# Output-weight maxima moved into the third head and a wait, last squares cut in two, residual rows loaded earlier

## The reference: what is computed

```
o = rms_norm(o_f + o_b, norm_g)          # per head of 128, HGRN2 group, 4 heads
o = o * silu(hgate)
y = concatenate([o_hg, o_att]) @ w_out   # (1152 x 1024) @ (1024 x 1024)
x = layer_norm(ALPHA * x + g2 * y, ln_g[1], ln_b[1])
x = layer_norm(ALPHA * x + 0.5 * g3 * swiglu(x * (1 + sc3) + sh3, ...), ln_g[2], ln_b[2])
```

## Time and profile before

| | |
|---|---|
| median of 3 runs | 2874.22 us (2873.36 to 2875.57) |
| the profiled execution | 2877.72 us, its span 2875.8 us |
| PE busy | 2614.7 us (91%) |
| DVE busy | 1979.7 us (69%) |
| ACT busy | 814.0 us (28%) |
| mean granted TensorE clock | 0.951 of full |

### The profile page before, as it was taken

How to read it: one execution, slowest core, us unless ns; L and a number is a source line. 1 busy time by engine, 2 the same in 40 slices (tenths; PEclk the granted TensorE clock), 3 DMA queues, 4 the chain that set the end, 5 groups by cost and what they waited for, 6 DMA issues and landing times. The chain is left out here.

```text
span 2875.8 us, 37783 instructions
## 1 busy us (share of the span) xinstructions
PE 2614.7 (91%) x15240; PEld 1631.2 (57%) x15240; DVE 1979.7 (69%) x2871; ACT 814.0 (28%) x1196; POOL 158.4 (6%) x191
## 2 busy tenths in 40 slices
PE   6899999999998867888699999868989999999996
PEld 6655555555554656766566666533545555555553
DVE  2577777778668666777455765668787777777768
ACT  0511111111211436666442242231311121111220
POOL 0000000000000220111200110101100000000003
PEclk9999999999998989999799999879999999999998
DMA  6323222322112110000110100022111111111001
GB/s 228 103 81 95 93 92 95 99 92 88 44 53 67 52 43 1 1 1 1 35 39 12 35 16 38 26 77 83 47 58 48 48 46 44 44 44 44 29 15 66
DMA packets 147786, 159.79 MB, mean 56 GB/s; under 512 B 8087, under 2 KB 125107, under 8 KB 146626
## 3 DMA queue, kind: packets, MB, share of 16 engines
q1 hardware_dynamic: 147650, 157.89, 17.2%
HBM read 147.74 MB, written 10.12 MB: 55 GB/s over the span
## 5 line engine op out<-in xcount | busy, mean ns | idle before, releaser
L1303 PE MATMUL psum<-act_hi,ffn_win_hi 128*128 128x384 f16 x2112 | 691.6, 327 | 2.0 <-DVE ffn_h_even L1610 2.0
L1303 PE MATMUL psum<-act_lo,ffn_win_hi 128*128 128x384 f16 x2112 | 691.4, 327 | 0.0
L1303 PE MATMUL psum<-act_hi,ffn_win_lo 128*128 128x384 f16 x2112 | 691.3, 327 | 0.0
L1474 ACT ACTIVATE ffn_silu<-psum,ffn_win_inverse 128x384 f32<-128x384 f32 x132 | 76.4, 579 | 1040.7 <-PE psum L1303 1038.8
L1645 DVE SCALAR_TENSOR_TENSOR Y<-psum,ffn_h_unit,Y 128x512 f32<-128x512 f32 x342 | 253.2, 749 | 120.9 <-PE psum L1334 118.9
L1334 PE MATMUL psum<-ffn_wout_hi,ffn_h_hi 128*128 128x512 f16 x792 | 309.1, 390 | 22.9 <-DVE Y L1128 12.3
L1334 PE MATMUL psum<-ffn_wout_hi,ffn_h_lo 128*128 128x512 f16 x792 | 308.3, 389 | 0.0
L1334 PE MATMUL psum<-ffn_wout_lo,ffn_h_hi 128*128 128x512 f16 x792 | 308.3, 389 | 0.0
L1303 PEld LDWEIGHTS psum<-act_hi,ffn_win_hi 128*128 128x128 f16 x2112 | 207.6, 98 | 138.6 <-DVE ffn_h_even L1610 2.4
L1303 PEld LDWEIGHTS psum<-act_hi,ffn_win_lo 128*128 128x128 f16 x2112 | 207.4, 98 | 138.1 <-issue 2.5
L1303 PEld LDWEIGHTS psum<-act_lo,ffn_win_hi 128*128 128x128 f16 x2112 | 207.5, 98 | 136.8 <-issue 2.3
(11 more groups left out here) (325 smaller groups left out, 4433.2 us busy)
## 6 DMA issues: line engine op xcount, KB each, us to landing
ffn_win_raw<-in_w_in SPq DMA_DIRECT2D x88, 512.0 KB, 5.1
w_mod<-in_w_mod SPq DMA_DIRECT2D x36, 1024.0 KB, 5.0
ffn_wout_raw<-in_w_out SPq DMA_DIRECT2D x44, 512.0 KB, 4.1
scan_w_raw<-in_w_mix SPq DMA_DIRECT2D x20, 512.0 KB, 5.3
x_after<-Y SPq DMA_DIRECT2D x9, 512.0 KB, 2.6
mixout_residual<-x_after SPq DMA_DIRECT2D x9, 512.0 KB, 3.4
Y<-in_x_sample SPq DMA_DIRECT2D x8, 512.0 KB, 6.7
ffn_residual<-in_x_sample SPq DMA_DIRECT2D x8, 512.0 KB, 3.3
```

The source lines that it names most:

```text
L1303: last = nc.tensor.matmul(bank[:, 0:CH], win[b][w][:, half, k, :], K.A[a][:, k, c * CH:(c + 1) * CH], start=(n == 0), stop=(n == 3 * KT - 1))
L1474: nc.scalar.activation(sa[s][:], pa[s][:, 0:CH], ACT.Silu, scale=winv[:, b:b + 1]).then_inc(silu, 1)
```

## The change

Five edits, all without a change of what is computed. (1) The maxima of output-weight blocks 0, 2, 3 and then 1, 4 are taken in the third head, those of 5, 6, 7 behind the last head. (2) A new `last_norm` replaces `norm` for the last head: it multiplies by the gate first, takes the three maxima and makes the weights' powers of two, and then waits for the root. (3) ACT squares the last head's first 768 tokens before the last tile is in, and PE's third unit waits for the second part. (4) The residual tiles have a place of their own (that of `ffn_wout_gated`, which is first written later), and tiles 0 and 1 are loaded right behind the first rows. (5) The second norm's rows are waited for and scaled behind tile 5 instead of ahead of tile 0.

```diff
@@ class MixOut @@
         for v in range(2):
             sp.dma_start(self.gate[:, v, :], ...).then_inc(self.rows, 16)
         sp.dma_start(self.gR[:], K.ln_g[0:1, :].broadcast_to([P, D])).then_inc(self.rows, 16)
         sp.dma_start(self.bR[:], K.ln_b[0:1, :].broadcast_to([P, D])).then_inc(self.rows, 16)
+        for t in range(2):
+            self.load_residual(sp, t)
 
     def load_late(self, sp):
         sp.wait_ge(self.w_lo, KT)
-        for t in range(2):
-            self.load_residual(sp, t)
         sp.dma_start(self.gB[:], ...).then_inc(self.affine_rows, 16)
         sp.dma_start(self.bB[:], ...).then_inc(self.affine_rows, 16)
...
     def splits_hi(self, act):
-        act.wait_ge(self.w_scale, 1)
...
     def splits(self, dve):
-        link(nc.vector.tensor_scalar(self.wq[:].bitcast(I32), self.wmax.bitcast(I32), EXPONENT, None, ALU.bitwise_and))
-        link(nc.vector.tensor_scalar(self.wq[:], self.wq[:], TINY, FULL, ALU.max, ALU.mult))
-        link(nc.vector.tensor_tensor(self.otops[:], self.omax, self.wq[:], ALU.mult))
+        link(nc.vector.tensor_tensor(self.otops[:], self.omax, self.wq, ALU.mult))
         nc.vector.tensor_reduce(self.otop[:], self.otops[:], AX_X, ALU.max).then_inc(self.o_max, 1)
-        nc.vector.reciprocal(self.ws[:], self.wq[:]).then_inc(self.w_scale, 1)
...
         dve.wait_ge(self.rows, 64)
-        dve.wait_ge(self.affine_rows, 32)
-        for rows in (self.gR, self.bR, self.gB, self.bB):
+        for rows in (self.gR, self.bR):
             link(nc.vector.tensor_scalar(rows[:], rows[:], ALPHA, None, ALU.mult))
...
             self.residual(dve, t + 3)
-            if c == 1:
+            if c == 0:
+                dve.wait_ge(self.affine_rows, 32)
+                for rows in (self.gB, self.bB):
+                    self.link(self.nc.vector.tensor_scalar(rows[:], rows[:], ALPHA, None, ALU.mult))
+            else:
                 self.affine(dve, 0)
             self.unit(dve, t + 2)
@@ hgrn_phase @@
+        mix_parts = ((0, 2, 3), (1, 4), (5, 6, 7))
...
                 for c in range(NCH):
+                    if h == HGH - 1 and c == NCH - 1:
+                        pe.wait_ge(sq_s, h + 2)
...
             def squares(h):
+                cut = 2 * CH if h == HGH - 1 else 0
+                if cut:
+                    act.wait_ge(oe_s, h * RPH + RPH)
+                    nc.scalar.activation(nb[:, 0:cut], acc[:, 0:cut], ACT.Square).then_inc(sq_s, 1)
                 act.wait_ge(oe_s, h * RPH + RPH + 1)
-                nc.scalar.activation(nb[:], acc[:], ACT.Square).then_inc(sq_s, 1)
+                nc.scalar.activation(nb[:, cut:], acc[:, cut:], ACT.Square).then_inc(sq_s, 1)
...
+            def last_norm(h):
+                dve.wait_ge(sq_s, h + 2)
+                link(nc.vector.scalar_tensor_tensor(acc[:], acc[:], K.cols[:, C_HGN + h:C_HGN + h + 1], K.O[:, h, :], ALU.mult, ALU.mult))
+                link(mix_weight_max(2))
+                link(nc.vector.tensor_scalar(K.mix_wq.bitcast(I32), K.mix_wmax.bitcast(I32), EXPONENT, None, ALU.bitwise_and))
+                link(nc.vector.tensor_scalar(K.mix_wq, K.mix_wq, TINY, FULL, ALU.max, ALU.mult))
+                link(nc.vector.reciprocal(K.mix_ws, K.mix_wq))
+                dve.wait_ge(rs_s, h + 1)
+                link(nc.vector.tensor_tensor(K.O[:, h, :], acc[:], nb[:], ALU.mult))
+                link(out_max(h))
...
                 row_max(n + 1, 0, V_, F0)
-                mix_weight_max(h, 0, 1)
+                if h == HGH - 2:
+                    mix_weight_max(0)
                 states(h, 0, 1, 0, 1)
...
                 gates(n, 0)
-                mix_weight_max(h, 6)
+                if h == HGH - 2:
+                    mix_weight_max(1)
                 states(h, 1, 1, 2, 3)
```

More of the change, by code:

```diff
@@ L2831, in out_max, with mix_weight_max @@
                 for k in tiles:
-                    largest(nc, K.mix_omax[:, k:k + 1], K.O[:, k, :])
-            def mix_weight_max(h, *tiles):
-                if h < HGH - 1:
-                    return
-                for k in tiles:
-                    dve.wait_ge(mix_in[k // NBLK], 16 * (KT - NBLK if k >= NBLK else NBLK))
-                    largest(nc, K.mix_wmax[:, k:k + 1], K.mix_raw[k][:])
+                    last = largest(nc, K.mix_omax[:, k:k + 1], K.O[:, k, :])
+                return last
+            def mix_weight_max(part):
+                dve.wait_ge(mix_in[part], 16 * len(mix_parts[part]))
+                for k in mix_parts[part]:
+                    last = largest(nc, K.mix_wmax[:, k:k + 1], K.mix_raw[k][:])
+                return last
+            def last_norm(h):
[8 more added lines that the diff above has]
+                link(out_max(h))
             def scan_head(h):
@@ L2917, in _ @@
                 scan_head(h)
-            norm(HGH - 1)
+            last_norm(HGH - 1)
 def rope_tables(np):
@@ L2970, in program @@
                  for k in range(KT)]
-    K.mix_omax, K.mix_wmax = K.cols[:, C_BMOD:C_BMOD + KT], K.cols[:, C_BMOD + KT:C_BMOD + 2 * KT]
+    K.mix_omax, K.mix_wmax, K.mix_wq, K.mix_ws = (K.cols[:, C_BMOD + i * KT:C_BMOD + (i + 1) * KT] for i in range(4))
     with ExitStack() as ctx:
```

35 lines of the change are left out of this document (16 added, 19 removed).

## The result

The changed kernel takes 2857.42 us (median of 4 runs, 2856.13 to 2858.33) beside 2873.79 us of the kernel before (4 runs): ratio 0.9938, 95% interval 0.9926 to 0.9950, a gain of 16.4 us. It was timed twice more with the experiments: 15.9 and 17.7 us less than the kernel before. The forecast was 13.1, a median of 2861.1 us in a range from 2856.5 to 2866.0. Both traces are laid over one another here, term by term. First the opening of the last FFN phase: after's SP queue, DVE from the last low half on, and PE's first half tile behind the pause (timelines; they answer to the earlier trace rows).

What follows compares the result with a forecast made beforehand. It took a DMA of the second norm's shift row to bound the stretch changed, with mostly PE from the first FFN group on. -8.85 + 0 - 0.95 - 2.8 - 0.5 = -13.1 us gave 2861.1 us, range 2856.5 to 2866.0.

Steps and rivals of the forecast that it cites:

- wait for rows: Output projection: DVE's 7.38 us wait goes whole and two of four scalings leave the path, -8.85 us.
- behind it, to the FFN: After PE's shortened pause: clock falls as before, so 0 us gained, with bounds 0 and 1.1.
- third head: Maxima moved here delay states and products: +3.6 us for three, +0.2 us for two more.
- last head: Maxima removed here shorten PE's waits for DVE's states: -4.75 us, bounds -3.6 and -7.2.
- last norm: End of the scan: earlier sums and root bring DVE's last multiplication forward, -2.8 us; -3.2 at full clock.
- opening: Two of DVE's little steps leave the path to `o_scale`, ahead of ACT's high halves: -0.5 us.
- rival 2: Third head costs less or last head gives more than 4.75: up to -3 us more, 2858; chance 0.10.
- rival 1: PE's clock holds through the short pause in the output projection: -14.2 us, 2860.0; chance 0.13.
- Rival 5: Longer third-head pause leaves PE at 1.2 GHz for later blocks, 3.8 us each: 2880; chance 0.02.
- Rivals 3, 4 and 6: Heads give nothing back, 2864.8, chance 0.12; FFN weights late, 2865, 0.07; most of the wait for rows kept, 0.04.

Runs made afterwards that it cites:

- slack: Changed kernel with both groups of maxima in the third head moved back to where DVE waits; 2855.89 us, in a later comparison 2856.69 beside the changed kernel's 2856.82.
- sixth_back: Changed kernel with one extra maximum on DVE in the last head, at the seventh maximum's old place; 2857.93 us.
- dose0: Changed kernel with all three of the third head's first group of maxima behind the delayed states, second group unmoved; 2853.02 us.
- dose1: Changed kernel with one of the third head's first three maxima ahead of the delayed states, two behind them; 2859.67 us.
- dose2: Changed kernel with two of the third head's first three maxima ahead of the delayed states, one behind them; 2860.47 us.
- slack_late: slack with the second norm's row scalings behind `unit` of tile 5 instead of ahead of it; 2856.38 us.
- rows_only: Kernel before with only the early residual loads to their own place and the second norm's rows waited for and scaled behind tile 5; 2866.03 us beside 2875.22.
- whole_squares: Changed kernel with the last head's squares in one piece again; 2858.48 us.
- sixth_right: Changed kernel with one extra maximum on DVE in the last head, at the sixth maximum's own old place; 2856.70 us beside 2856.82.
- scan_only: Changed kernel with residual loads and row scalings where they were, keeping moved maxima, new last norm and split squares; 2864.31 us, ratio 0.9967.

## Why the prediction was right and wrong

Term by term, against the first trace of before and, where it differs, the second:

| term | forecast | measured |
|---|---|---|
| wait for rows | -8.85 | -8.92; -8.50 |
| behind it, to the FFN | 0 | -0.8; +0.3 |
| third head | +3.8 | +3.58 |
| last head | -4.75 | -8.33 |
| last norm | -2.8 | -3.34 |
| opening | -0.5 | -0.27 |
| sum | -13.1 | -18.1; -16.6 |

The measured time lies inside the range, 3.7 us below the forecast. The second sum is the one that the timed gains (16.4, 15.9, 17.7) bear out; the first trace of before stands 3.5 us above its median, which the forecast took for a shift that is the same for both.

**The step that failed is the last head's term, -4.75 with bounds -3.6 and -7.2.** Its work was right: 2.25 us for the first two maxima (forecast 2.4, but at the wrong wait: the one that ends at 1861.85 grew from 2.11 to 2.79 us, and the one that shrank stands ahead of it, 6.01 us before and 3.75 after), 1.20 for the next two (13.06 to slack's 11.86; forecast 1.15), 1.13 for the sixth (forecast 1.2), nothing for the seventh (sixth_back): 4.58 us in all. The other 3.75 us are PE's clock: 1.93 and 0.85 at 2 to 3 and 3 to 4, where it comes back a stretch earlier, and 0.95 at 4 to 5, where it no longer falls. The forecast saw half clock in these rows and counted it as a thing of the kernel that stays where it is, even as a reason why only 1.15 of 2.4 us come back; it had no term for a clock that moves when the times do. My bound of -7.2 was made from DVE's work alone, 8.33 lies beyond it, and the time came out below what I gave to rival 2, whose condition (the last head gives more than 4.75) is what happened. The runs show that the clock is the difference, and that it is repeatable up to the fifth `masked`; they do not show what moves it or how it could have been foreseen: dose0, dose1, dose2 and slack moved the same maxima and got 0.0, +3.9, +6.5 and +3.1 us from it, in their traces, beside the work that they moved. This is the wait of the kernel before that shrank (timeline of PE, last head):

```profile
1853.35 3.75 PE L2503 MATMUL psum<-scan_v_blocks,ke_turned 128*128 128x512 f32 x4 [6.01 <-DVEq L2820]
```

**The wait for rows** went as worked out, including its 3.98 us from the first scaling to the first `gated` (3.97 in the trace); the FFN loads moved back cost nothing. **Behind it** I chose 0 by the wrong reason. I took a fallen clock for certain, from pauses of 2.11 to 2.47 us. The changed kernel's clock stayed up, which is the condition of rival 1. Its 1.1 us are there against the first trace of before, with 14 slow products and 97.05 us to the FFN; slack_late, without the scalings on the way, has 95.94. But the clock has to hold only in part for that: the second trace of before, with 7 slow products, already has 95.95, and rows_only, whole_squares and four others had 8 or 9 slow products behind the same pause of 2.44 us and kept the changed kernel's 96.25. Edit 5's scalings cost 0.3 us where I had none, which makes -0.8 against the first trace and +0.3 against the second.

The Trainium skill (TensorE: Matmul & The Clock Gate, Why this matters for your kernels), that short gaps leave the clock alone, is borne out by the changed kernel and sixth_right and contradicted by rows_only and the earlier trace rows, with pauses equal to 0.03 us. The Trainium skill (TensorE: Matmul & The Clock Gate, Part 1: The HAM clock gate) says that the monitor runs free of the kernel, so that the point of change varies with where the work falls. The last head, where kernels 0.2 us apart ahead of it differ by 2.8 us, would fit that, and so would scan_only, where the clock fell behind the fifth `masked` and in the same order elsewhere did not. That seven traces of one order agree to 0.02 us up to there is not what it leads one to expect, and no run here explains it.

**Third head:** right in mechanism, 1.13 us a maximum and not 1.2, since a row of three lasts 3.47. **Last norm:** the bound -3.2 for full clock, with DVE as the limit, is what happened, with 3.34 us. The forecast's own sum was also 0.2 us short: with the sums ending at 1908.1 and the last logarithm 0.6 us behind, as in the earlier trace rows, its rows give -3.0 and not -2.8. **Rival 5**, the low clock in the third head's blocks, did not occur in the changed kernel, but dose1 and dose2 had a small form of it (1.7 and 1.2 us). **Rivals 3, 4 and 6** did not occur: the heads gave back more, and no load was late.

## What to carry to other kernels

Where PE runs at half clock in stretches, price a change twice, by the work that it moves and by the slow stretches near it, and widen the range by what they hold (here 3.75 us of 33), in both directions. Then try neighbouring orders: dose0, whose third head differs from slack's by 0.2 us, is the fastest kernel of this study, 3.8 us below the changed one. And work belongs where its engine waits anyway: three maxima cost 3.4 us ahead of a state that PE waits for, and none behind it.

## What I had not expected of the hardware

- One pause does not tell what the clock does: behind 2.47 us four updates ran at half clock in two traces of before and at the full clock in sixth_right; behind 2.44 us there were 0, 8 or 9 slow products, depending on the kernel.
- The clock can also fall where PE is busy throughout: 0.90 over 16.68 us in dose1, 1.00 in dose0 at the same work, 1.7 us apart.
- In the last head up to the fifth `masked` the pattern repeated to 0.02 us in seven traces of one order. It is not fixed everywhere: behind that, scan_only took 7.16 us for the norm where the changed kernel took 6.56, with the same order in the scan. Only one run of each timing was traced.
- DVE's wait for the same DMA of rows was 6.96 and 7.38 us in the two traces of the kernel before, and 10.25 us in scan_only.
- No gap stood behind a table load, as the earlier trace rows already had it: the load at 1904.53 lasted 1.28 us, and the exponential started at 1905.82.
